# A fused hybrid layer (RG-LRU, windowed attention, gated ConvFFN) on one core: another order for the first loop step, the modulation sums, the attention unit and the second norm

## What is computed

```python
mod_x = silu(c) @ w_mod + b_mod                      # six vectors of 1024: sh1, sc1, g1, sh2, sc2, g2
hx = rms_norm(x, norm1_w) * (1 + sc1) + sh1          # the context hc likewise, from c_ctx
rx, rgx, qx, kx, vx, gax, gbx = split(hx @ w_in)     # 1024, 1024, 1024, 256, 256, 1024, 1024 columns
xc = dwconv(rx, width 4)
r, i = sigmoid(xc @ gate_a), sigmoid(xc @ gate_x)    # 16 blocks of 64, both directions
y_rx = (scan_forward + scan_backward) * gelu(rgx)
p = exp(q k^T - max) over 3 key blocks of 128 and 256 context keys, with a sink logit per head
y_ax = (p / (sum(p) + exp(sink - max))) @ v
merged = sigmoid(gax) * (y_rx @ w_o_rnn) + sigmoid(gbx) * (y_ax @ w_o_attn)
x1 = x + g1 * (merged @ w_out)
hx2 = rms_norm(x1, norm2_w) * (1 + sc2) + sh2
out = rms_norm(x1 + g2 * conv_ffn(hx2), final_norm_w)
```

## Time and profile before

| | |
|---|---|
| median of 3 runs | 1845.27 us (1842.65 to 1847.67) |
| the profiled execution | 1846.12 us |
| its span in the trace | 1844.3 us |
| PE busy | 1753.3 us, 95% of the span |
| DVE, ACT, POOL busy | 1226.3, 701.0, 562.6 us |
| granted TensorE clock, mean | 0.984 of full speed |
| chain that ended last | PE 76%, DVE 10%, issue 4%, POOL 3%, ACT 3%, DMA 2% |

### The profile page before, as it was taken

One profiled execution on the slowest core, in us unless ns is written; L12 is line 12 of the kernel. 1 busy time (PEld: TensorE's weight loads), 2 busy tenths in 40 slices (PEclk: granted clock), 3 DMA queues, 4 the chain that ended last, 5 costly groups with the idle time before them and its releaser, 6 DMA issues.

```text
span 1844.3 us, 22712 instructions
## 1 busy us (share of the span) xinstructions
PE 1753.3 (95%) x8148; PEld 1453.3 (79%) x8148; DVE 1226.3 (66%) x1377; ACT 701.0 (38%) x899; POOL 562.6 (31%) x264
## 2 busy tenths in 40 slices
PE   3998999999999899989999979999999999999997
PEld 1887888888788688878888747888888888888886
DVE  7975667668516477764116989999999998514423
ACT  4235555567201178850002025444444444202212
POOL 2025666666345475634545730000000000000000
PEclk8999999999999999999999989999999999999999
DMA  9231111211335200033115721222212224523112
GB/s 378 61 109 38 49 49 49 65 49 41 137 124 169 75 1 0 0 110 119 68 68 222 290 80 58 91 91 80 96 74 80 91 80 153 204 95 124 65 46 92
DMA packets 53084, 178.43 MB, mean 97 GB/s; under 512 B 10528, under 2 KB 10912, under 8 KB 51872
## 3 DMA queue, kind: packets, MB, share of 16 engines
q1 hardware_dynamic: 46208, 157.17, 23.8%
q10 hardware_dynamic: 6816, 20.45, 3.4%
HBM read 141.42 MB, written 30.93 MB: 93 GB/s over the span
## 4 chain that ended last, share of the span: by engine, by line
PE 76%; DVE 10%; issue 4%; POOL 3%; ACT 3%; DMA 2%; ACTq 0%; SPq 0%; DVEq 0%; POOLq 0%
PE acc L873 15%; PE acc L874 15%; PE acc L875 15%; PE gp L873 10%; PE gp L875 10%; PE gp L874 10%; DVE pt_lo L2169 1%; POOL wlo_both L704 1%; POOL whi_both L702 1%; POOL ssum L855 1%; DMA wst<-in_w_in 1%; ACT pt_hi L1308 1%; DVE hx_lo L2072 1%; DMA wgr<-in_mod_rest 1%; ACT prob L1308 1%
## 5 line engine op out<-in xcount | busy, mean ns | idle before, releaser
L873 PE MATMUL acc<-hx_hi,whi_both 128*128 128x512 f32 x672 | 263.5, 392 | 19.9 <-DVE hx_lo L1912 14.9
L874 PE MATMUL acc<-hx_lo,whi_both 128*128 128x512 f32 x672 | 262.5, 391 | 0.0
L875 PE MATMUL acc<-hx_hi,wlo_both 128*128 128x512 f32 x672 | 262.2, 390 | 0.0
L702 POOL TENSOR_TENSOR whi_both<-wst,ones 128x1024 fp32r<-128x1024 f32 x58 | 156.0, 2689 | 268.2 <-PE acc L875 235.4
L704 POOL TENSOR_TENSOR wlo_both<-wst,whi_both 128x1024 fp32r<-128x1024 f32 x58 | 178.9, 3084 | 4.6
L873 PEld LDWEIGHTS acc<-hx_hi,whi_both 128*128 128x128 f32 x672 | 126.7, 189 | 49.5 <-DVE hx_lo L1912 16.2
L875 PEld LDWEIGHTS acc<-hx_hi,wlo_both 128*128 128x128 f32 x672 | 126.6, 188 | 26.7
L874 PEld LDWEIGHTS acc<-hx_lo,whi_both 128*128 128x128 f32 x672 | 126.7, 189 | 25.3
L873 PE MATMUL acc<-T_hi,fac_hi 128*128 128x512 f32 x264 | 102.8, 389 | 0.3 <-DVE fac_lo L2365 0.3
L875 PE MATMUL acc<-T_hi,fac_lo 128*128 128x512 f32 x264 | 102.7, 389 | 0.0
L874 PE MATMUL acc<-T_lo,fac_hi 128*128 128x512 f32 x264 | 102.7, 389 | 0.0
(11 more groups left out here) (353 smaller groups left out, 4668.1 us busy)
## 6 DMA issues: line engine op xcount, KB each, us to landing
wst<-in_w_in SPq DMA_DIRECT2D x43, 512.0 KB, 3.4
wst<-in_w_up SPq DMA_DIRECT2D x26, 512.0 KB, 4.0
wgr<-in_mod_rest SPq DMA_DIRECT2D x6, 2048.0 KB, 12.5
ffn_row_scratch<-ca SPq DMA_DIRECT2D x24, 512.0 KB, 2.6
wst<-in_w_down SPq DMA_DIRECT2D x32, 384.0 KB, 3.1
g_in<-ffn_row_scratch SPq DMA_DIRECT2D x24, 512.0 KB, 6.4
wup<-in_w_up SPq DMA_DIRECT2D x22, 512.0 KB, 3.8
wmod<-in_mod_first SPq DMA_DIRECT2D x16, 512.0 KB, 15.2
```

What stands on the lines that cost most here:

```text
L702: nc.gpsimd.tensor_tensor(whi[s][:, 0:kc, :], wst[s][:, 0:kc, :], ones_of(kc), mult).then_inc(S["w_hi"], 1)
L873: mm(out_ap, w_h, x_h, start=first, stop=False)
L874: mm(out_ap, w_h, x_l, start=False, stop=False)
L875: return mm(out_ap, w_l, x_h, start=False, stop=last)
```

## The change

Four parts.

1. **First loop step.** TensorE's order becomes half 0 of the rx product of chunk 1, gate 0, context row, gate 1, the first four input chunks of half 1, gate 2, the last four, gate 3, and then the whole rgx product (before: half 1 in one piece ahead of gate 2, and gate 3 between the two halves of the rgx product). VectorE puts off the two last rotary instructions of key head 1 until after the split of the convolved chunk. ScalarE's first gelu waits only on the reads of what it overwrites; the store of key head 1 and the wait for the four stores move behind the second gate sigmoid, and the centre tap of chunk 1 behind the third. GpSimd splits the next rx weights inside `gated_input(0, 0)` instead of ahead of it.
2. **Modulation sums.** 24 instead of 8 sums are made in the merge stage (6 before `merge` 0, 8 before `merge` 1, 8 before 2, 2 before 3) with blocks that ACT's queue loads into the same three slots; merges 2 and 3 leave the loop. The first `merge_gate` moves behind six loads, of which the last three wait on sums 0 to 2. In the output stage 8 sums are left (groups 6 and 7, at products 1 and 2), from two slots; the loads of groups 2 to 5 leave SP's queue.
3. **Attention unit.** VectorE: max 0, max 1, low block 0, max 2, low blocks 1 and 2, max 3, sink term, low blocks 3 and 4, denominators (before: low blocks 0 to 2 ahead of max 2, low block 3 ahead of max 3, then low block 4 and the sink term). ScalarE: high block 0 comes between the first two exponentials, blocks 1 and 2 ahead of the third, 3 and 4 ahead of the fourth. TensorE multiplies block 0 with the values ahead of the transposes of block 4.
4. **Second norm.** The sums over channels are made in columns: each of 8 token blocks of `ssum` is the stationary operand against two columns of ones, and likewise the squares of the last chunk, 16 small fp32 matmuls. VectorE adds the two parts, ScalarE takes the root of 128x4 values, VectorE their reciprocal and a diagonal of 128x512 from them, and one fp32 matmul of ones with the diagonal spreads it over the partitions. `normed` reads the factor from PSUM. ScalarE calls one Sqrt on a constant ahead of the last squares.

The diff, cut to its core:

```diff
@@ sync: load_groups, output stage
             def load_groups(g):
-                if g >= 5:
-                    sp.wait_ge(S["rest_acc"], KC + NG * (g - 4))
-                sp.dma_start(wgr[(g - 2) % 3][:, :, :], in_rest[g]).then_inc(wr_loaded[(g - 2) % 3], 16)
+                s = g - EARLY_SUMS // NG
+                sp.dma_start(wgr[s][:, :, :], in_rest[g]).then_inc(wr_loaded[s], 16)
...
-            load_groups(2)
             load_out(3)
-            load_groups(3)
+            load_groups(6)
+            load_groups(7)
...
-                if m < 6:
-                    load_groups(m + 2)
@@ gpsimd
+            def next_weights():
+                split_gates(1)
+                split_w(W_S1 + 2, last_use=A_S1 + 2)
...
-                    split_w(W_S1 + 2, last_use=A_S1 + 2)
-                    gated_input(0, 0, between=1)
+                    gated_input(0, 0, between=next_weights)
@@ tensor: first_step, weigh, attention, second norm
                 gate(0, 1)
-                half(A_S1 + 2, W_S1, 1, hx_hi, hx_lo).then_inc(S["acc_full"], 1)
-                gate(0, 2)
+                part, s = slice(HALF, SEQ), W_S1 % 2
+                for ks in (range(KQ), range(KQ, KC)):
+                    for k in ks:
+                        last = three(acc[(A_S1 + 2) % 2][:, part], whi[s][:, k, :], wlo[s][:, k, :],
+                                     hx_hi[:, k, part], hx_lo[:, k, part], k == 0, k == KC - 1)
+                    if ks[0] == 0:
+                        gate(0, 2)
+                last.then_inc(S["acc_full"], 1)
+                gate(0, 3)
                 weights(W_S1 + 1)
                 slot_free(A_S1 + 3)
                 half(A_S1 + 3, W_S1 + 1, 0, hx_hi, hx_lo)
-                gate(0, 3)
                 half(A_S1 + 3, W_S1 + 1, 1, hx_hi, hx_lo).then_inc(S["acc_full"], 1)
...
+            def flip_and_weigh(n, kh, u):
+                flip(n, kh, u, 3)
+                weigh(n, kh, u, [0])
+                flip(n, kh, u, 4)
+                weigh(n, kh, u, [1, 2, 3, 4])
...
+            def square_column(columns, m, src):
+                return mm(columns[:, 2 * m:2 * m + 2], src[:, P * m:P * (m + 1)], ones[:, 0:2], start=True, stop=True)
+
+            for m in range(XT):
+                last = square_column(early_columns, m, ssum)
+            last.then_inc(S["st_full"], 1)
             for h in range(2):
                 pe.wait_ge(S["sq_last"], h + 1)
-                mm(stat[h], ones[:, :], sqb[:, HALF * h:HALF * (h + 1)], start=False, stop=True)\
-                    .then_inc(S["acc_full" if h else "st_full"], 1)
+                for m in range(4 * h, 4 * h + 4):
+                    last = square_column(late_columns[h], m, sqb)
+                last.then_inc(S["st_full"], 1)
+            for h in range(2):
+                pe.wait_ge(S["st_diag"], AT["st_diag"] + h + 1)
+                mm(stat[h], ones[:, :], diag[h].rearrange("p t n -> p (t n)"), start=True, stop=True)\
+                    .then_inc(S["acc_full" if h else "st_spread"], 1)
@@ scalar: chunk step 1, attention, merge stage
+                else:
+                    store_key(1)
+                    act.wait_ge(S["ksv_stored"], 16 * 4)
+                    gate_sigmoid(0, 2)
+                    centre(1, e)
...
                 exp_head(n, kh, u, 0)
+                if before:
+                    high_block(*before, 0)
                 exp_head(n, kh, u, 1)
                 if before:
-                    for j in range(4):
-                        high_block(*before, j)
+                    high_block(*before, 1)
+                    high_block(*before, 2)
                 exp_head(n, kh, u, 2)
                 if before:
+                    high_block(*before, 3)
                     high_block(*before, 4)
...
-            merge_gate(A_S4, 0, 0, None)
             row_again(0)
             for j in range(3, 6):
                 load_g1(j)
+            merge_gate(A_S4, 0, 0, None)
+            for j in range(6, 14):
+                load_g1(j)
             merge_gate(A_S4, 1, 1, (S["row_silu"], 1))
-            for j in range(6, KC):
+            for j in range(14, 22):
                 load_g1(j)
@@ vector: output stage, second norm
-                if 1 <= m < 7:
-                    add_group(m + 1)
+                if 1 <= m < 3:
+                    add_group(m + 5)
...
-                                       in1=rstd[:, part], op0=mult, op1=mult).then_inc(S["n2_a"], 1)
+                                       in1=stat[h], op0=mult, op1=mult).then_inc(S["n2_a"], 1)
...
-                v.reciprocal(rstd[:, part], rstd[:, part]).then_inc(S["st_rstd"], 1)
...
+                v.reciprocal(four, rms[:, 4 * h:4 * h + 4]).then_inc(S["st_rstd"], 1)
+                dve.wait_ge(S["st_rstd"], AT["st_rstd"] + h + 1)
+                v.tensor_tensor(diag[h][:, :, :], ident[:, :].rearrange("p (o n) -> p o n", o=1).to_broadcast([P, XT // 2, P]),
+                                four.rearrange("p (t o) -> p t o", o=1).to_broadcast([P, XT // 2, P]), mult)\
+                    .then_inc(S["st_diag"], 1)
```

More of the change, by code:

```diff
@@ L67 @@
 A_ST2 = 59
+EARLY_SUMS = 24
 def rope_tables():
@@ L234, in build @@
     ssum = sb("ssum", B + 110592, [P, SEQ])
-    rstd = sb("rstd", B + 98304, [P, SEQ])
+    diag = [sb(f"diag{h}", B + 98304 + 2048 * h, [P, XT // 2, P]) for h in range(2)]
     def block(name, off):
@@ L427, in build @@
         att_out = acc[1][:, HALF:SEQ]
+        stat = [acc[A_ST2 % 2][:, HALF * h:HALF * (h + 1)] for h in range(2)]
+        early_columns, late_columns = gp[:, HALF:HALF + 16], [gp[:, HALF * (2 + h):HALF * (2 + h) + 16] for h in range(2)]
         def block_base(n, u):
@@ L1143, in flip, with weigh @@
                 last.then_inc(S["pt_full"], 1)
-            def weigh(n, kh, u):
+            def weigh(n, kh, u, blocks):
                 nb = 4 if is_edge(n) else 5
-                pe.wait_ge(S["v_s"], 2 * u + 2)
-                if not (isinstance(u, int) and u == 0):
-                    pe.wait_ge(S["o_read"], u)
+                if blocks[0] == 0:
+                    pe.wait_ge(S["v_s"], 2 * u + 2)
+                    if not (isinstance(u, int) and u == 0):
+                        pe.wait_ge(S["o_read"], u)
                 o = att_out
                 base = block_base(n, u)
-                for j in range(nb):
+                for j in blocks:
+                    if j >= nb:
+                        continue
                     pe.wait_ge(S["pt_lo_s"], base + j + 1)
@@ L1171, in attention @@
                 if before:
[L1172 to L1176, removed]
+                    flip_and_weigh(*before)
+            units(pe, attention, lambda n, kh, u: ([flip(n, kh, u, j) for j in range(3)], flip_and_weigh(n, kh, u)))
             pe.wait_ge(S["o_read"], N_KV * XT)
@@ L1654, in _ @@
                 load_g1(j)
+            merge_gate(A_S4, 0, 0, None)
+            for j in range(6, 14):
+                load_g1(j)
             merge_gate(A_S4, 1, 1, (S["row_silu"], 1))
-            for j in range(6, KC):
+            for j in range(14, 22):
                 load_g1(j)
-            with act.Fori(1, KC // 2) as i:
+            merge_gate(A_S4, 2, 0, (S["merged"], 1))
+            for j in range(22, EARLY_SUMS):
+                load_g1(j)
+            merge_gate(A_S4, 3, 1, (S["merged"], 2))
+            with act.Fori(2, KC // 2) as i:
                 for s in range(2):
@@ L2176, in attention @@
                 if before:
-                    for j in range(3):
-                        low_block(*before, j)
+                    low_block(*before, 0)
                 maxima(n, kh, u, 2)
                 if before:
+                    low_block(*before, 1)
+                    low_block(*before, 2)
+                maxima(n, kh, u, 3)
+                sinks(n, kh, u)
+                if before:
                     low_block(*before, 3)
-                maxima(n, kh, u, 3)
-                if before:
                     low_block(*before, 4)
@@ L2226, in _ @@
             row_product(0)
-            for j in range(3):
+            for j in range(6):
                 add_g1(j)
             merge(0, 0)
-            for j in range(3, 6):
+            for j in range(6, 14):
                 add_g1(j)
+            rest_bias(0, 1)
             merge(1, 1)
-            for j in range(6, KC):
+            for j in range(14, 22):
                 add_g1(j)
-            dve.wait_ge(S["rest_acc"], KC)
-            rest_bias(0, 1)
-            with dve.Fori(1, KC // 2 - 1) as i:
+            merge(2, 0, 1)
+            for j in range(22, EARLY_SUMS):
+                add_g1(j)
+            merge(3, 1, 1)
+            with dve.Fori(2, KC // 2 - 1) as i:
                 for s in range(2):
```

62 lines of the change are left out of this document (36 added, 26 removed).

## The result

The changed kernel takes 1823.61 us (median of 4 runs, 1821.91 to 1824.90), the kernel before 1845.24 beside it. The ratio is 0.9882 with an interval of 0.9865 to 0.9900: faster by 21.6 us (1.2%), where the forecast was 33.6 and its range ended at 1822. The profiled execution of after is the fastest of its four (1821.91, span 1820.1), that of before lies above its median, so the two traces are 24.3 apart.

What follows compares the result with a forecast made beforehand. TensorE, busy nearly all the time, was taken as the bound, so only its idle stretches could be won: 12.0 - 0.9 + 4.2 + 9.3 + 9.0 = 33.6 us, giving 1811.7 against the median; range 1804 to 1822, eight in ten.

Steps and rivals of the forecast that it cites:

- The terms given for low block 4: Attention unit: VectorE's steps put low block 4 at 6.7 us, so a unit takes 9.6, 0.7 less.
- The first rival: Attention: flips and scalings hold the unit through high block 0, so it wins 3 us instead of 9; chance 0.15.
- edge units less: Attention: units at the ends win less, within 9.0 us for 14 units with their neighbours' prices.
- (a): First loop step: rotary instructions moved behind the split end gate 0's 3.3 us wait and its slow start, 4.9 won.
- slow start: First loop step: TensorE at half clock after idling costs 1.6 us; a remaining wait of 1 was taken not to bring it.
- (b): First loop step: gate 3 moved early covers 18.2 of ScalarE's 19.1 us chain; wins 5.5 plus a slow start of 1.6.
- The cover of the key store: First loop step: the store's landing ahead of gate sigmoid 2 was taken to lose nothing, 1.2 us at the other end.
- The wait for sg at the third product: Merge stage: the first sigmoid stands behind a load waiting on sum 2, a new wait of 0.9 us.
- 1 of it returns: Output stage: of 4.2 us won, 1 is lost again if group 6 lands over 1 late behind a weight load.
- the 6.8 estimated: Second norm: 16 column matmuls with four weight loads each by the skill's rule, 2 us above the 4.8 taken; part wins 7.3.
- the slow case: Attention falls to the low clock; four such units cancel the win, six give 1870 us; chance 0.02.
- no change: First step and norm wins are met again by chains of other engines, as ScalarE's chunk chain; chance 0.03.

Runs made afterwards that it cites:

- e1: Changed kernel with VectorE's sink term moved back behind low blocks 3 and 4: 1812.34 us, ratio 0.9821 to the kernel before.
- e10: Changed kernel with unread filler matmuls on TensorE, 26 ahead of gate 1 of chunk 1 and 8 behind the norm's column sums: 1819.47 us.
- e6: Changed kernel with the first merge sigmoid ahead of the load of block 5 and the last group of sums at output product 4: 1823.01 us.
- e5: Changed kernel with gate 3 of chunk 0 put back between the two halves of the rgx product: 1827.64 us.
- e8: Changed kernel with GpSimd's low part of the next weights held until VectorE has made the first diagonal: 1823.99 us.
- e9: Changed kernel with sink term last, merge sigmoid, last sums and GpSimd's low part moved, key head 1 stored ahead of the second gate sigmoid: 1810.13 us.
- e13: Changed kernel with each of the eight early column sums of the second norm made four times over: 1827.16 us.

## Why the prediction was wrong

**Attention: the step that failed is the addition.** The part's steps were nearly right and their sum was not. The terms given for low block 4, from low block 0 at 2.4 on (0.6, 0.8, 1.2, 0.8, 1.0, 0.6), add up to 7.4, not to the 6.7 that I wrote; 7.4 is where it starts today, and in the trace after it starts 6.8 + 0.6 behind the first maximum. Read rightly, the sum said that a unit would not change: the signal and the sink term, 0.9 ahead of low block 3, take back what the earlier high block 0 gives. What the rows before could not show is that 0.5 of that 0.9 is a wait for GpSimd's q_lo. The first rival was nearer in size, but it named flips and scalings as the chain, and e1 shows that they held nothing. The 5.8 that did come is at the edge units and behind them, which I had only as "edge units less", and 2.1 of it came with the clock. That the stage came out within the part's range of 4 to 14 is luck.

**First step, the largest error in us (7.0 for 12.0).** (a) Right: wait and slow start ended, and gate 0 to gate 1 with the half before is 5.1 shorter, forecast 4.9. (b) The step that failed is the chain of 19.1 kept as it was. It ran beside a VectorE that had its split done before; now cast, low part and radicands follow each other while GpSimd is busy, and the roots wait 2.9. The second step is the slow start: I took a wait of 1 not to bring it, and with 4.1 it came, 1.7. The cover of the key store had 0.4 of a loss (other end 1.2): its landing, 139.6 to 145.5, is 5.9 for 640 KB, near the 5.6 of the loads, which I had halved; the other store of that size, 127.8 to 130.8, took 2.9. So 2.0 instead of 7.1. The rule behind it stands in the Trainium skill (SBUF — State Buffer, Who interferes with whom): a VectorE instruction in a mode that uses two ports, which casts can enter, or with two inputs in SBUF contends with a GpSimd instruction that reads SBUF, and the one that is first keeps the shared ports for its whole length; instructions with one such input in other modes do not contend. This case agrees: cast, low part, radicands and diagonal are about two to three and a half times as long beside GpSimd, the low part ends one own length behind GpSimd's instruction and the sink term with it, and the taps, which read PSUM, keep their 3.9.

**Merge and output stage.** The wait for sg at the third product is 0.7 with 0.16 more hidden, as forecast, and a group that lands late gave 0.6 back, the "1 of it returns" of the forecast. The five products behind the third are 0.13 to 0.26 late each, 0.8 in sum, with no wait of note; no run shows why. The part is 1.3 short of its 3.3.

**Second norm.** Right, 1.0 better than forecast. A column took 0.22, the lower end, not 0.3; the diagonal 1.7, not 0.7, beside GpSimd; spread and pace are as reckoned (28.4 for 28.5). The 107 ns a weight load of the Trainium skill (TensorE: Matmul & The Clock Gate, LDWEIGHTS) fits each pass (0.112) at the full clock, but a column has two weight loads, not four, so the 6.8 estimated with it is 3.4. Two shown passes do not mean two streams, though: in e10, at the lower clock, a pass of the spread takes 0.85 from start to start, twice the 0.43 of a filler of as many columns. With 6.8 the sum would have been 31.6, and the verdict the same.

**The range.** It ended at a win of 23.2. In the traces 9.3 of the 33.6 are missing: 5.0 in the first step, 3.2 in attention (5.3 with the clock as in e6), 1.3 in merge and output stage, 0.7 in stages that should not have changed, less 1.0 won at the norm. The medians miss 12.0, since the traced execution is the fastest of its four. The lower ends of the five parts, added up, win 17.3 (9 - 3.9 + 3.2 + 5 + 4), which is 1828: the range took for granted that the parts would not fall short together, and with the sum for low block 4 right attention's 9.0 was not there to begin with. The slow case and "no change" were rightly put low.

## What to carry to other kernels

Add up a hand-laid schedule twice, and against the row where the same event lies today: if the sum gives the old time, the reordering has only exchanged one wait for another. A duration from the trace holds only beside the neighbours it had there; when an instruction with two SBUF inputs moves next to GpSimd's work, add to its own length what is left of the GpSimd instruction that it meets (up to 2.3 here), however short it is itself. A small instruction that nobody waits for, as the sink term with its 0.16, costs that, its wait for GpSimd (0.5) and its signal (0.21) when it stands ahead of the one instruction that everybody waits for: moving it back brought 11.3, half as much as the whole change had brought.

## What was not expected of the hardware

TensorE's clock fell to its lower level in the middle of unbroken work: rows of fp32 matmuls of two columns, each with its own weight load (e5, e6, e8, e9, e10 and e13; a pass 0.112 at 2.4 GHz, 0.213 at 1.2). In the changed kernel itself the fall came just behind them. And such a fall can turn an earlier start into nothing, as in e8. Matmuls put into a wait of 4.1 kept the clock up and won 1.8 (e10); put behind the columns, where it had fallen already, they cost 1.9. And with the same code the clock was not the same: behind a wait of 2.0 in the changed kernel 485 to 505 us had 0.91, behind one of 2.1 in e13 it had 1.00, and in the second attention unit it came back sooner in some traces than in others. That moved a stage by 1.5 to 2.1 with no edit in it, so a win of that size in one trace is first to be held against the granted clock of the stage.
